# Joint hi and lo passes for three of the seven products of a feed-forward group, with the up slab's remainder on GpSimd

## The reference

```python
D_MODEL = 1024; SEQ = 512; DEPTH = 2; FFN_DIM = 2816

def swiglu(x, w_gate, w_up, w_down):
    return (jax.nn.silu(x @ w_gate) * (x @ w_up)) @ w_down

for i in range(DEPTH):
    x = layer_norm(DN_ALPHA * x + 0.5 * swiglu(x, ffn1_w_gate[i], ffn1_w_up[i], ffn1_w_down[i]), ...)
    ...  # mixer and cross attention, each with its layer_norm
    x = layer_norm(DN_ALPHA * x + 0.5 * swiglu(x, ffn2_w_gate[i], ffn2_w_up[i], ffn2_w_down[i]), ...)
```

## Time and profile before

| what | value |
|---|---|
| median of three runs | 2186.6 us |
| span of the profiled execution (first to last instruction) | 2184.3 us |
| TensorE matmul busy | 2161.4 us, 99% |
| VectorE, ScalarE, GpSimd busy | 1334.5, 1068.6, 779.0 us |
| matmuls | 13640 |
| mean granted TensorE clock | 0.999 |

### The profile page before, as it was taken

One profiled execution on the slowest core, in us unless ns is written; L12 is line 12 of the kernel. 1 busy time (PEld: TensorE's weight loads), 2 busy tenths in 40 slices (PEclk: granted clock), 3 DMA queues, 4 the chain that ended last, 5 costly groups with the idle time before them and its releaser, 6 DMA issues.

```text
span 2184.3 us, 35402 instructions
## 1 busy us (share of the span) xinstructions
PE 2161.4 (99%) x13640; PEld 1918.4 (88%) x13640; DVE 1334.5 (61%) x2315; ACT 1068.6 (49%) x1927; POOL 779.0 (36%) x573
## 2 busy tenths in 40 slices
PE   9999999999999999999999999999999999999998
PEld 8999998878888989898899999887778887989896
DVE  7656667464436928385766666657655346747475
ACT  4434345563435525254643534466654445535353
POOL 3201116567638030305420111555548555120203
PEclk9999999999999999999999999999999999999999
DMA  4323334213313333333232333320004312333332
GB/s 152 122 93 95 110 113 134 77 49 109 123 39 107 107 97 108 95 110 123 87 118 96 97 107 114 119 79 29 20 11 132 110 49 77 116 97 96 108 97 78
DMA packets 58199, 207.50 MB, mean 95 GB/s; under 512 B 6960, under 2 KB 7088, under 8 KB 57264
## 3 DMA queue, kind: packets, MB, share of 16 engines
q1 hardware_dynamic: 56016, 197.68, 28.9%
q10 hardware_dynamic: 2016, 7.55, 0.9%
HBM read 203.10 MB, written 2.10 MB: 94 GB/s over the span
## 4 chain that ended last, share of the span: by engine, by line
PE 93%; DVE 3%; ACT 1%; POOL 1%; issue 1%; DMA 0%; DVEq 0%; ACTq 0%
PE bank L1772 14%; PE bank L1773 14%; PE bank L1774 14%; PE bank L1983 11%; PE bank L1988 11%; PE bank L1985 11%; PE bank L2184 2%; PE bank L2145 2%; PE bank L2117 1%; PE bank L2118 1%; PE bank L1872 1%; PE bank L1874 1%; PE bank L1873 1%; PE bank L1791 1%; PE bank L1802 1%
## 5 line engine op out<-in xcount | busy, mean ns | idle before, releaser
L627 POOL TENSOR_TENSOR w_lo<-w_raw,w_hi 128x1024 fp32r<-128x1024 f32 (+1 forms) x226 | 530.1, 2354 | 1175.3 <-ACT w_hi L804 1175.2
L1772 PE MATMUL bank<-h_hi,w_hi 128*128 128x512 f32 x960 | 377.8, 394 | 1.5 <-DVE h_lo L1751 0.8
L1773 PE MATMUL bank<-h_lo,w_hi 128*128 128x512 f32 x960 | 374.4, 390 | 0.0
L1774 PE MATMUL bank<-h_hi,w_lo 128*128 128x512 f32 x960 | 373.8, 389 | 0.0
L804 ACT ACTIVATE w_hi<-w_raw 128x1024 fp32r<-128x1024 f32 (+1 forms) x227 | 230.4, 1021 | 130.5 <-PE bank L1774 92.4
L1772 PEld LDWEIGHTS bank<-h_hi,w_hi 128*128 128x128 f32 x960 | 180.3, 188 | 45.5 <-issue 3.3
L1774 PEld LDWEIGHTS bank<-h_hi,w_lo 128*128 128x128 f32 x960 | 180.2, 188 | 38.2
L1773 PEld LDWEIGHTS bank<-h_lo,w_hi 128*128 128x128 f32 x960 | 180.5, 188 | 34.2
L1983 PE MATMUL bank<-x_hi,w_hi 128*128 128x256 f32 x864 | 139.6, 284 | 0.3
L1772 PE MATMUL bank<-x_hi,w_hi 128*128 128x512 f32 x352 | 139.2, 396 | 0.0
L1988 PE MATMUL bank<-x_hi,w_lo 128*128 128x256 f32 x864 | 138.9, 283 | 0.0
(11 more groups left out here) (307 smaller groups left out, 5036.0 us busy)
## 6 DMA issues: line engine op xcount, KB each, us to landing
w_raw<-w_dram SPq DMA_DIRECT2D x315, 512.0 KB, 3.5
w_raw<-w_dram SPq DMA_DIRECT2D x64, 448.0 KB, 3.3
f<-mem_dram ACTq DMA_DIRECT2D x5, 1024.0 KB, 5.2
out_dram<-t SPq DMA_DIRECT2D x8, 256.0 KB, 2.2
t<-x_dram SPq DMA_DIRECT2D x2, 512.0 KB, 6.9
f<-cmp_w_dram ACTq DMA_DIRECT2D x1, 1024.0 KB, 4.9
t<-x_dram ACTq DMA_DIRECT2D x2, 256.0 KB, 5.5
t<-x_dram ACTq DMA_DIRECT2D x1, 512.0 KB, 8.1
```

What stands on the lines that cost most here:

```text
L627: pool.tensor_tensor(w_lo[:, slot(s), 0:n * P], w_raw[:, s % RAW, 0:n * P], w_hi[:, slot(s), 0:n * P].bitcast(F32), ALU.subtract).then_inc ...
L1772: pe.matmul(dst, w_hi[:, slot(s), w], m_hi[:, k, :], start=k == 0, stop=False)
L1773: pe.matmul(dst, w_hi[:, slot(s), w], m_lo[:, k, :], start=False, stop=False)
L1774: last = pe.matmul(dst, w_lo[:, slot(s), w], m_hi[:, k, :], start=False, stop=k == n - 1)
```

## The change

Prod6, prod5 and prod3 become joint. A new function runs the first two passes as one: each chunk's weights hi are loaded once and multiplied by 512 columns, the activations' hi (256) beside their lo (256), which for this lie in one tensor `x`. The result takes both halves of the bank: the left as ever, the right a sum of its own for the lo pass. So 12 matmuls of 256 columns become 4 of 512 and 4 of 256. Prod1, prod2, prod4 and prod7 stay as they are.

The halves have to be added. ScalarE's `keep2` and `keep3` now copy the right half, and VectorE adds the left one to the copy (`join2`, `join3`); prod5 waits for joined2 and prod3 for joined3, where snap2 and snap3 stood. After prod3 ScalarE copies the right half (`right_last`), VectorE adds the left (`join_last`), and Silu runs in SBUF (`silu_second`). GpSimd does `up_rest` for all groups but the first of each part, after VectorE's `late_rest` of the same group. The orders on ScalarE and VectorE are rewritten. The rest of the diff merges semaphores of the set-up phase.

```diff
-        x_hi = sb("x_hi", [P, KC, SEQ], F32R)
-        x_lo = sb("x_lo", [P, KC, SEQ], F32R)
+        x = sb("x", [P, 2, KC, SEQ], F32R)
+        x_hi, x_lo = x[:, 0], x[:, 1]
...
+            def up_rest(g):
+                hi, rest = w_up(g)
+                pool.wait_ge(up_hi, g.count + 1)
+                pool.wait_ge(late_lo, g.count + 1)
+                pool.tensor_tensor(rest, raw_half(g.up, 1), hi.bitcast(F32), ALU.subtract).then_inc(up_lo, 1)
...
                 for part in range(len(FPARTS)):
+                    for g in st.groups[part][1:]:
+                        up_rest(g)
                     feed(st.out[part][-1])
...
                 def keep2(g):
                     act.wait_ge(m6, g.count + 1)
-                    act.activation(snaps(g, 1), bank_a(g)[:, 0:256], ACT.Copy).then_inc(snap2, 1)
+                    act.activation(snaps(g, 1), bank_a(g)[:, 256:512], ACT.Copy).then_inc(snap2, 1)
...
-                def silu_second(g):
+                def right_last(g):
                     act.wait_ge(m3, g.count + 1)
                     act.wait_ge(z["hidden"], st.p0 + g.pair - 1)
-                    act.activation(gated[g.pair % 2][:, half[1]], bank_a(g)[:, 0:256], ACT.Silu).then_inc(z["gated"], 1)
+                    act.activation(gated[g.pair % 2][:, half[1]], bank_a(g)[:, 256:512], ACT.Copy).then_inc(last_right, 1)
+
+                def silu_second(g):
+                    act.wait_ge(last_out, g.count + 1)
+                    own = gated[g.pair % 2][:, half[1]]
+                    act.activation(own, own, ACT.Silu).then_inc(z["gated"], 1)
...
                     for g in mine:
-                        if before and before is not begin:
-                            keep3(before)
                         if g is not begin:
                             keep1(g)
                         if g.next:
                             gate_round(g.next)
-                        if before:
-                            silu_second(before)
-                        keep2(g)
+                        if g is begin:
+                            keep2(g)
+                        elif before:
+                            right_last(before)
                         if g.next:
                             pair_round(g.next, 0)
-                            if g is begin:
-                                keep3(g)
+                        if g is begin:
+                            keep3(g)
+                        else:
+                            if before:
+                                silu_second(before)
+                            keep2(g)
+                        if g.next:
                             pair_round(g.next, 1)
+                            up_round(g.next)
                         else:
                             feed(st.out[part][0])
+                        if g is not begin:
+                            keep3(g)
                         if before:
                             hi(before.pair, before.first)
                         silu_first(g)
-                        if g.next:
-                            up_round(g.next)
                         before = g
...
+                def join2(g):
+                    dve.wait_ge(snap2, g.count + 1)
+                    dve.tensor_tensor(snaps(g, 1), snaps(g, 1), bank_a(g)[:, 0:256], ALU.add).then_inc(joined2, 1)
...
                     for g in mine:
-                        if before:
-                            up2(before)
                         if g.i == 1:
                             first(g)
                         if g.next:
...
                             sums_second(g.next)
+                        if before:
+                            join_last(before)
+                        if g.next:
                             if g is not begin:
                                 gate_rest(g.next)
+                        join2(g)
+                        if g.next:
                             pair_rest(g.next)
-                        if before:
-                            up1(before)
                         if g.next:
                             late_rest(g.next)
                         if before:
+                            up1(before)
+                        join3(g)
+                        up2(g)
+                        if before:
                             lo(before.pair, before.first)
-                        if g.next:
-                            up_rest(g.next)
                         before = g
...
+            def quarter_joint(g, w, i, both, begin, rest, done):
+
+                hi, lo = w
+                a = bank_a(g)[:].rearrange("p (h s) -> p h s", h=2)
+                columns = [slice(512 * i + P * k, 512 * i + P * k + P) for k in range(4)]
+                for k, c in enumerate(columns):
+                    pe.matmul(a, hi[:, c], both[:, :, k, :], start=begin and k == 0, stop=False, skip_group_check=True)
+                pe.wait_ge(*rest)
+                for k, c in enumerate(columns):
+                    last = pe.matmul(a[:, 0, :], lo[:, c], both[:, 0, k, :], start=False, stop=k == 3, skip_group_check=True)
+                last.then_inc(done, 1)
...
                 def prod5(g):
                     if g.n == 0:
                         pe.wait_ge(comb_lo, c0 + 4)
-                    pe.wait_ge(snap2, g.count + 1)
+                    pe.wait_ge(joined2, g.count + 1)
                     pe.wait_ge(pair_hi, 2 * g.count + 2)
-                    quarter(bank_a(g)[:, 0:256], w_pair(g, 1), 0, comb[1], False, (late_lo, g.count + 1), m5)
+                    quarter_joint(g, w_pair(g, 1), 0, x[:, :, 0:4, half[1]], False, (late_lo, g.count + 1), m5)
```

More of the change, by code:

```diff
@@ L374, in build @@
                 4: (t4[0], t4[1])}
+        rows_joint = ra[:, 0:2048].rearrange("p (h k s) -> p h k s", h=2, k=4)
         lng = sb("lng", [P, NLN, KC])
@@ L411, in build @@
         pool_set = sem("pool_set")
-        iota_done = sem("iota_done")
         dist_f = sem("dist_f")
@@ L1487, in up2, with up1, join3, join_last @@
                 def up2(g):
-                    dve.wait_ge(snap3, g.count + 1)
-                    dve.wait_ge(m7, g.count + 1)
-                    dve.tensor_tensor(bank_b(g)[:, half[1]], snaps(g, 2), bank_b(g)[:, half[0]], ALU.add).then_inc(up2_out, 1)
-                def up1(g):
-                    dve.wait_ge(snap2, g.count + 1)
-                    dve.wait_ge(m4, g.count + 1)
-                    dve.tensor_tensor(bank_b(g)[:, half[0]], snaps(g, 1), bank_b(g)[:, half[0]], ALU.add).then_inc(up1_out, 1)
-                    dve.wait_ge(up1_out, g.count + 1)
-                    hid(g.pair, bank_b(g)[:], -0.5)
+                    dve.wait_ge(joined3, g.count + 1)
+                    dve.wait_ge(m7, g.count + 1)
+                    dve.tensor_tensor(bank_b(g)[:, half[1]], snaps(g, 2), bank_b(g)[:, half[0]], ALU.add).then_inc(up_out, 1)
+                def up1(g):
+                    dve.wait_ge(joined2, g.count + 1)
+                    dve.wait_ge(m4, g.count + 1)
+                    dve.tensor_tensor(bank_b(g)[:, half[0]], snaps(g, 1), bank_b(g)[:, half[0]], ALU.add).then_inc(up_out, 1)
+                    dve.wait_ge(up_out, 2 * g.count + 2)
+                    hid(g.pair, bank_b(g)[:], -0.5)
+                def join2(g):
+                    dve.wait_ge(snap2, g.count + 1)
+                    dve.tensor_tensor(snaps(g, 1), snaps(g, 1), bank_a(g)[:, 0:256], ALU.add).then_inc(joined2, 1)
+                def join3(g):
+                    dve.wait_ge(snap3, g.count + 1)
+                    dve.tensor_tensor(snaps(g, 2), snaps(g, 2), bank_a(g)[:, 0:256], ALU.add).then_inc(joined3, 1)
+                def join_last(g):
+                    own = gated[g.pair % 2][:, half[1]]
+                    dve.wait_ge(last_right, g.count + 1)
+                    dve.tensor_tensor(own, own, bank_a(g)[:, 0:256], ALU.add).then_inc(last_out, 1)
                 begin = st.groups[0][0]
```

32 lines of the change are left out of this document (16 added, 16 removed).

## The result

| what | before | after |
|---|---|---|
| median | 2186.6 us (2184.2 to 2186.8, 4 runs) | 2203.6 us (2201.3 to 2205.1, 4 runs) |
| span of the profiled execution | 2184.3 us | 2201.8 us |
| mean granted TensorE clock | 0.999 | 0.993 |

A forecast was written before the change was run, and what follows sets the result against it. TensorE, 99% busy, was taken as the bound. Joint products -12.2, blocks' starts +14.3 and later parts' starts +6.4 sum to +8.5 us: span 2192.8 plus 2.3 around it gives 2195.1 us, range 2189.5 to 2205.

The forecast's parts named there:

- TensorE bounds, and each wait is paid: Whole kernel: TensorE is 99% busy, so a change pays what it takes off TensorE's stream less each wait added.
- The wait at a block's start: First group of each of four blocks: prod5 waits 3.68 us for join2, and 0.10 more behind it.
- The small wait ahead of product 3: First group of a block: prod3 waits 0.29 us for join3, and 0.10 more behind it.
- the sum +8.5: Whole kernel: -12.2 from joint products, +14.3 at blocks' starts, +6.4 at later parts' starts, giving 8.5 us slower.
- the joint step: Joint products: a 512-column matmul takes 0.2266 us, a product 1.386 instead of 1.44, saving 12.2 us in all.
- rival (a): Behind the four block-start waits TensorE's clock falls, adding 6.6 to 13.2 us: 2202 to 2208; chance 0.11.
- The 2.3 us around the span: Profiled execution: the median has 2.3 us around the span, added to 2192.8 to give 2195.1.
- rival (d): Joint products: the joint matmul saves nothing, two pieces costing a step of 0.2400 us: 2207.3 us; chance 0.06.
- Steady groups: Middle of a part: VectorE works 9.46 of 9.92 us, up_rest on GpSimd costs nothing, and TensorE does not wait.
- Rival (c): Steady groups: VectorE becomes the bound as GpSimd's up_rest costs over 0.46 us a group: 2203 or 2227; chance 0.06.
- Later parts' starts: First groups of the eight other parts: TensorE waits 0.70 and 0.10 us for join2, 6.4 us in all.
- rival (b): Starts: VectorE is in time, so not slower: 2171.4 us, or 2186 with block starts costing 1.5; chance 0.09.

The follow-up runs named there:

- e4_filled: The changed kernel with 15 unused 128-column matmuls on TensorE ahead of product 5 of a block's first group; 2198.0 us.
- e8_gpsimd_alone: The kernel before with only up_rest moved to GpSimd, for all groups but the first of a part; 2186.1 us, ratio 0.9999.
- e6_one_piece: The changed kernel with joint matmuls reading 512 neighbouring columns instead of two pieces of 256, on wrong data; 2202.9 us in one run.
- e3_all_starts: The changed kernel with first groups of blocks and later parts reordered so join2, and at blocks join3 and up2, come earlier; 2189.0 us, ratio 1.0012.
- e7_rest_on_vector: The changed kernel with up_rest back on VectorE, behind lo, for every group; 2204.6 us, ratio 1.0085.
- e2_part_starts: The changed kernel with keep2 and join2 earlier in the first group of each later part only; 2197.1 us, ratio 1.0044.
- e1_join2_first: The changed kernel with join2 of a block's first group ahead of the prologue's last remainders and sums; 2198.4 us, ratio 1.0051.
- e5_two_plain: The changed kernel with each block's first two groups plain, their up_rest on VectorE, and keep2 and join2 earlier at later parts' starts and throughout first parts; 2183.3 us.

## Why the prediction was right and where it was wrong

**TensorE bounds, and each wait is paid.** Right. The ledger closes to within 0.4 us by TensorE's rows alone.

**The wait at a block's start.** Right in place, cause and length: 3.54 to 3.59 shown, 3.68 and 0.10 forecast, `join2` 0.61 after the start of the last sum. The walk assumed that nothing upstream moves, and nothing did. The small wait ahead of product 3 was right too (0.30 in e4_filled). Measured at full clock, the sum +8.5 with the joint step corrected is +11.6, and e4_filled has 2198.0 - 2186.9 = 11.1.

**The clock. This is the step that failed.** The sum had no term for it, and the case stood as rival (a) with a chance of 0.11, "Against it: no row shows a fall, and the mean clock is full". That was no evidence: the waits of the kernel before were all shorter than the new ones (1.6 us at most), so its trace had nothing to say of a wait of 3.7. Nor was the clock full: the first us, ran at half clock, which the record of the granted clock does not cover there, and other executions fall in the mixer too (e8_gpsimd_alone). A case that a wait outside the seen range makes possible is not made unlikely by a trace that never went there. The rival's size, 6.6 to 13.2 us, was taken from the kernel's first us and was too high: measured 5.0 to 5.5 (e4_filled). Its time of 2202 to 2208 held the result all the same, because the joint products gave 3.1 less than forecast. The forecast by itself was 2192 to 2198 and missed; the stated range held 2203.6 only because it reached into rival (a), and there a price too high and a gain too high made up for each other. That is luck in the size; the direction and the waits were not. The point forecast was off by 8.5.

**The 2.3 us around the span.** In every run since, an execution's time is 1.7 to 1.9 us above its own span (2203.6 against 2201.8 for the changed kernel's profiled one), so 2.3 is not what an execution has around it. The forecast does not rest on it: the median of 2186.6 and 8.5 give the same 2195.1.

**The joint step.** Mis-sized: 0.2325 in place of 0.2266, 1.40 in place of 1.386 a product, 9.1 us in place of 12.2. "I take 0.2266, the rows of the same width" came from a run of 36 equal matmuls, and the joint ones stand four at a time between matmuls of 256. The worry of the prediction, the operand in two pieces, was the wrong one (e6_one_piece). Why the place costs 0.006 a step stays open. Of rival (d), that the joint matmul saves nothing, about a quarter came true (3.1 of 12.2).

**Steady groups.** Right. VectorE works 9.39 us a group (9.46 forecast) of 9.96, and no wait follows. GpSimd's 64 subtractions last 1.30 each and all but one overlap only VectorE operations with one operand in PSUM, which keep their 0.42 and 0.69. The one, in block two's second group, made a sum of weights take 0.95 in place of 0.68, the 0.3 us that the prediction had. The Trainium skill, page "SBUF — State Buffer", section "Who interferes with whom", says that a VectorE instruction with two SBUF inputs contends with a GpSimd instruction that reads SBUF. The traces agree where such an operation did stand next to one (1.69 for 0.68 in e3_all_starts). Where the move was made alone, the kernel's time did not change (e8_gpsimd_alone, ratio 0.9999). What the prediction did not see is that the move was not needed either: e7_rest_on_vector costs 1.1 by the medians. Rival (c) was well away.

**Later parts' starts.** Right: 6.4 forecast, 6.5 when taken away (e2_part_starts), 6.4 by the ledger.

**Not slower, rival (b).** Its condition, VectorE 3.7 us earlier at a block's start, is what e1_join2_first and e3_all_starts tried by order alone. The first brought `join2` in time and was late with `join3`, the second brought both in time and was late in the second group. e5_two_plain, which takes the joins out of the first two groups, is the one without such a wait.

## What to carry to other kernels

A new wait of TensorE is to be priced with what its clock may do behind it, above all where the wait is longer than any in the trace at hand: the trace can't argue against what it never tried. One trace is one draw of the clock: before two spans are compared to a few us, compare their first us and the stretches that the change leaves alone. Before reordering an engine to take a wait away, add up its work from the last point where it was on time to the place of the wait; if that sum is too long, the wait only moves, and the work must shrink or stay out of that stretch. Take the price of an instruction from rows with the same neighbours, not only of the same size.

## What the runs showed of the hardware

- The granted clock fell to half around idle stretches of TensorE of 2.5 to 3.6 us at 20 of 24 block starts, in the six traces that have such a wait. It stayed full at the others: behind 3.54 (e2_part_starts) and 3.56 (e6_one_piece), 2.72 (e1_join2_first) and 2.52 us (e3_all_starts).
- The fall came in the wait (blocks one and two of the changed kernel) or after work was taken up again, by 1.1 and 1.45 us in its blocks three and four. Half clock lasted into the work for 2.85 us (e7_rest_on_vector, block two) to 6.0 us (e1_join2_first, block three).
- Its net price was 1.97, 1.29, 0.90 and 0.86 us in the four blocks of one execution, for waits of the same length.
- It also fell without a long wait, in the mixer near 481, with idle stretches of 0.71 and 0.56 us ahead (e8_gpsimd_alone).
- The record of the granted clock can miss the kernel's first us: 1.00 before, where matmuls stepped by 0.43.
- Matmuls of 128 columns that compute nothing, filling the wait, kept the clock at 1.00 in all four blocks (e4_filled).
- Matmuls of 512 columns in fours between matmuls of 256 step by 0.2325 us, in a long run of their own by 0.2266.
- A moving operand in two pieces of 256 columns runs as fast as one piece of 512: 0.2325 a step both (e6_one_piece).
